# Chosen tokens by indirect DMA with a fifteenth weight slot, gate rows on four column groups, and a last feed-forward group added chunk by chunk

## The chip, the cores and the metric

The kernel runs on one core of a Trainium2 chip, as one program. The metric is device time in microseconds (us); the lower the better. The time before is the median of three runs.

## The reference

Two transformer blocks run one after the other on 512 tokens of width 1024, all in f32. The first is a token mixer (a gated scan, a convolution and attention, merged) followed by an expert-choice feed-forward. The second is pooling and a gated delta rule, cross attention, and a plain feed-forward. The parts that the change touches are these:

```python
def expert_choice_ffn(h, router_w, w_gate, w_up, w_down):
    cap = CAPACITY_FACTOR * n // N_EXPERTS          # 64 tokens for each of 16 experts
    aff = jax.nn.softmax((h @ router_w).astype(jnp.float32), axis=-1)
    w_sel, idx = lax.top_k(aff.transpose(0, 2, 1), cap)
    xs = jax.vmap(lambda hb, ib: hb[ib])(h, idx)
    hid = jax.nn.silu(jnp.einsum('becd,edf->becf', xs, w_gate)) * jnp.einsum('becd,edf->becf', xs, w_up)
    ys = jnp.einsum('becf,efd->becd', hid, w_down) * w_sel[..., None].astype(h.dtype)
    return jax.vmap(lambda yb, ib: jnp.zeros((n, d), h.dtype).at[ib.reshape(-1)].add(yb.reshape(-1, d)))(ys, idx)
...
        proj = hn @ w_in[l]                          # second block
        b = proj[..., P + 4 * W:P + 4 * W + H]       # gate rows: 4 columns
        a = proj[..., P + 4 * W + H:]                # and 4 more
...
        h = h + sqrelu_mlp(rmsnorm_2(h, norm_mlp_g[l]), w_up[l], w_down[l])
    return rmsnorm_2(h, final_norm_g)
```

## The kernel before

Every engine has one program, a list of steps at the end of the kernel (PE_STEPS, DVE_STEPS, ACT_STEPS, SP_STEPS, POOL_STEPS), and semaphores order them. Nothing is planned by cost: an engine runs its list in the order written, and a wait holds all that is behind it. TensorE is PE in the rows, VectorE DVE, ScalarE ACT, SyncE SP.

Weights come through one queue, SP's (`WeightStream.load`, line 164), unit by unit into slots. A unit waits until TensorE has counted up `weights_used` past the unit that had the slot before. For the experts there are fourteen slots of 1024 KB (`SLOTS`), eight in the ring and six in the columns of three branches that are done by then. A pair of experts takes 24 units (gate, up, down; four quarters; two experts), eight pairs 192.

`dve_router` computes affinities, turns them to 16 rows of 512 and finds the 64 largest of each row in eight rounds (line 1982 finds eight, line 1984 replaces them). It then makes of the replaced places a running count, the slot of each token (lines 1987 to 1993). `pe_router` turns that to tokens by experts, and `dve_hot` compares it with the slot numbers: `hot` holds one-hot columns of a pair's 2 x 64 tokens, `whot` the same times the affinity. `pe_gather` (line 2026) multiplies the tokens' rows `h2tok` by `hot`, four matmuls for each of eight chunks, in two halves; `act_gather` (line 2034) scales and shifts. `pe_hot_turn` (line 2045) and `act_hot_turn` turn `whot` for the way back.

`pe_experts` runs the pairs. A quarter of a matrix is eight matmuls for two experts side by side on 64 columns each (line 2169, x16 in the rows, since an f32 matmul stands as two). The way back, `pe_scatter` (line 2071), is one matmul for each of eight chunks and is mixed into the next pair's gate and up quarters; `dve_scatter` adds it to the stream. The gather of the next pair stands between the down quarters:

```python
                    pe_expert_quarter(pe, i, 2, q, 4, lambda e, k: e_hidT[:, k, CAP * e:CAP * e + CAP])
                    if q < 2 and i < PAIRS - 1:
                        pe_gather(pe, i + 1, q)
                    if q == 2:
                        pe_hot_turn(pe, i)
```

`pe_in2` is the second block's first projection. Its gate rows are eight matmuls with 36 columns (line 2356), one for each chunk of the width, then come pool products 2 and 3 (`product`, line 2347), the final norm's sum, the spread of the gate rows over the partitions (`pe_rows_spread`, lines 2385 and 2390), the pool mixes (`mix_pool`, line 2405) and the products of keys, queries and values. `act_in2` makes sigmoid, softplus and the spread's copy of them; `act_qkv_copy` (line 2449) takes each product out of PSUM, and `act_qkv_silu`, in turn with it, waits for VectorE's convolution. `dve_in2` scans the rows, runs pool 0 and the final scalings (line 2297), copies the turned columns (line 2491), and runs pools 1 to 3 before the convolutions (line 2552 on).

In `dve_mlp` the last down group is multiplied by the norm's factor (line 3284) and added to the stream (line 3286), two chunks at a time; ScalarE's squares (line 536) and TensorE's sums for the last norm (line 3316) follow.

Of the kernel before, what the change touches and what calls it, by code (L numbers as in the profile page):

```python
# [6 lines left out]
I32 = mybir.dt.int32  # L7
ALU = mybir.AluOpType
# [176 lines left out]
def mixed_block_kernel(nc, A, out):  # L185

    ctx = ExitStack()
    with ctx:
        sems = {}

        def sem(name):
# [5 lines left out]
            "pe_once": ['rows1_turned', 'rows_turned', 'router_bias', 'aff_turned', 'slots_turned', 'rows2', 'fin_sum', 'spread', 'columns'],  # L197
            "act_once": ['c_exp', 'aff_exp', 'dt_added', 'row_ln', 'fin_root', 'spread_copied', 'decays', 'row_exp'],
            "dve_once": ['silu_c', 'ht_sums', 'ct_sums', 'router_scaled', 'logits_out', 'logits_shifted', 'affinity', 'slots_row', 'mix_columns', 'pool_scaled', 'mix_folded', 'pools_rooted', 'fin_folded', 'row_sums', 'columns_copied', 'd_factors', 'differences', 'queries_out', 'q_decayed'],
# [12 lines left out]
        arena = ctx.enter_context(nc.sbuf_tensor("arena", [P, COLS], F32))  # L212
        psum = ctx.enter_context(nc.psum_tensor("psum", [P, 8, BANK], F32))
# [60 lines left out]
        ws = WeightStream([sem(f"weights_full_{u}") for u in range(14)], sem("weights_used"))  # L274
# [1491 lines left out]

        QUADS = [(0, 0), (0, 1), (3, 1), (2, 0), (1, 0), (2, 1), (3, 0)]
# [76 lines left out]
        hot = [pairwise.take(LT, P) for _ in range(2)]  # L1844
        xs = [ex.take(KC, P) for _ in range(2)]
        whot = [ex.take(LT, P) for _ in range(2)]
# [4 lines left out]
        slotT = rt.take(LT, NE)  # L1851
# [7 lines left out]
        top8 = rt.take(8, 8)  # L1859

# [40 lines left out]
        def pe_router(pe):  # L1901
# [34 lines left out]
        def act_router(act):  # L1936
            await_once(act, "logits_shifted")
            act.activation(aff, aff, ACT.Exp).then_inc(once("aff_exp"), 1)
            for at_, n in enumerate(HTOK_ORDER):
                act.wait_ge(sem("htok"), at_ + 1)  # L1940
                act.activation(h2tok[:, n // 2, (n % 2) * 512:(n % 2) * 512 + 512], psum[:, n % 4, :], ACT.Identity,
                               scale=r_col[:, n // 2:n // 2 + 1]).then_inc(sem("htok_out"), 1)

        def dve_router(dve):
# [36 lines left out]
            for r in range(CAP // 8):  # L1981
                dve.max(top8[0:NE, r, :], work[r % 2])
                dve.drain()
                dve.match_replace(work[(r + 1) % 2], top8[0:NE, r, :], work[r % 2], -1.0)
                dve.drain()
            chosen = row_b[0:NE, :]
            dve.tensor_scalar(chosen, work[0], 0.0, None, ALU.is_lt)
            dve.drain()
            dve.tensor_tensor_scan(row_work[0:NE, :], chosen, chosen, 0.0, ALU.add, ALU.max)
            dve.drain()  # L1990
            dve.tensor_tensor(row_work[0:NE, :], row_work[0:NE, :], chosen, ALU.mult)
            dve.drain()
            dve.tensor_scalar(row_a[0:NE, :], row_work[0:NE, :], 1.0, None, ALU.subtract).then_inc(once("slots_row"), 1)
            await_once(dve, "slots_turned")
            dve.tensor_copy(slotT, psum[:, 7, 0:LT * NE].rearrange("p (t e) -> p t e", t=LT))
            dve.drain()
            dve_hot(dve, 0)

        def dve_hot(dve, i):

            if i >= 2:
                dve.wait_ge(sem("gathered"), 2 * (i - 1))
                dve.wait_ge(sem("hot_turned"), i - 1)
            for t in range(LT):
                dve.tensor_tensor(hot[i % 2][:, t, :].rearrange("p (e c) -> p e c", e=2), bmid(slots, 2),
                                  bcast(slotT[:, t, 2 * i:2 * i + 2], CAP), ALU.is_equal)
            dve.drain()
# [344 lines left out]
        def pe_in2(pe):  # L2352
# [14 lines left out]
            for n in range(8):  # L2367
# [3 lines left out]
                if n == 0:  # L2371
                    mix_pool(pe, 1)
# [1048 lines left out]
```

## Time and profile before

| what | before |
|---|---|
| median of 3 runs | 2751.68 us (2750.51 to 2752.56) |
| profiled execution, its own time | 2754.7 us |
| its span | 2752.9 us |
| mean granted TensorE clock | 0.989 |
| TensorE busy | 2667.6 us (97%) |
| VectorE busy | 1303.1 us (47%) |
| ScalarE busy | 560.8 us (20%) |
| DMA, mean over the span | 136 GB/s |
| DMA packets | 328720, 374.66 MB |

The table is of the whole span; a stage can have another limit. A window gives, for a stretch, the busy time and instructions of TensorE, its weight loads, VectorE, ScalarE and POOL, then the granted clock of TensorE (1.00 is 2.4 GHz, 0.50 is 1.2 GHz) and what the DMA engines moved. The chain of waits is the chain of work that ended last. In a timeline the bracket behind a row is the time in which its engine was idle before it, with what ended that.

### The profile page before, as it was taken

To read this page: it belongs to the slowest core of one execution; us is meant where nothing else is said; L and a number is where in the kernel's file an instruction comes from. 1 tells how busy PE (TensorE), PEld (TensorE's weight loads), DVE (VectorE), ACT (ScalarE), POOL (GpSimd) and SP (SyncE) were. 2 spreads that over 40 slices of the span, in tenths; PEclk is the share of its full clock that TensorE was granted. 3 is DMA by queue.
4 is the path that set the end of the run, shared out by engine and by line. 5 is a ranking of instruction groups with operands and counts; after the bars stand their busy time and mean duration, and the time that the engine had idled before them with its cause. 6 is when DMAs were issued, how large, how long until landed. Compare 5 with 4: busy or idle time off the path is not lost.

```text
span 2752.9 us, 33182 instructions
## 1 busy us (share of the span) xinstructions
PE 2667.6 (97%) x13084; PEld 1873.1 (68%) x13084; DVE 1303.1 (47%) x2417; ACT 560.8 (20%) x942; POOL 170.4 (6%) x140
## 2 busy tenths in 40 slices
PE   6999999999899999999799999999999999999998
PEld 3788888887667666787443333334595877888887
DVE  4255665655465666645311111146473335654654
ACT  3121212222234344311111010122322113000001
POOL 0122211220000000232000000000000000000000
PEclk9999999999999999999899999999999999999999
DMA  9721212211111121235799999952103421233231
GB/s 334 236 62 53 61 43 56 61 30 38 39 47 54 54 62 42 82 90 178 281 409 409 409 409 409 409 178 61 31 1 87 132 73 47 77 92 92 80 89 46
DMA packets 328720, 374.66 MB, mean 136 GB/s; under 512 B 11073, under 2 KB 274070, under 8 KB 325270
## 3 DMA queue, kind: packets, MB, share of 16 engines
q1 hardware_dynamic: 328326, 371.93, 39.8%
q8 instruction: 84, 1.38, 0.2%
q10 hardware_dynamic: 272, 1.05, 0.1%
q14 instruction: 38, 0.31, 0.0%
HBM read 370.85 MB, written 2.10 MB: 135 GB/s over the span
## 4 chain that ended last, share of the span: by engine, by line
PE 89%; DVE 5%; DMA 2%; DVEq 1%; ACT 1%; issue 1%; SPq 0%; ACTq 0%; POOLq 0%; POOL 0%
PE psum L1782 29%; PE psum L2169 12%; PE psum L1462 7%; PE psum L2347 5%; PE psum L720 3%; PE psum L1129 2%; PE psum L2071 2%; PE psum L2026 2%; PE psum L815 2%; PE psum L728 2%; PE psum L2885 2%; PE psum L705 2%; PE psum L1318 2%; PE psum L1370 2%; PE psum L1347 2%; PE psum L2967 1%
## 5 line engine op out<-in xcount | busy, mean ns | idle before, releaser
L1782 PE MATMUL psum<-arena 128*128 128x256 f32 x4144 | 908.6, 378 | 1.9 <-DVEq L1805 1.1
L1782 PEld LDWEIGHTS psum<-arena 128*128 128x128 f32 x4144 | 777.8, 189 | 121.0 <-issue 10.0
L2169 PE MATMUL psum<-arena 128*64 128x512 f32 x1536 | 347.8, 597 | 5.1 <-DMA arena<-in_w_down 3.5
L2169 PEld LDWEIGHTS psum<-arena 128*64 128x64 f32 x1536 | 103.4, 136 | 220.8 <-issue 217.2
L1462 PE MATMUL psum<-arena 128*128 128x256 f32 x896 | 206.6, 381 | 0.0
L1462 PEld LDWEIGHTS psum<-arena 128*128 128x128 f32 x896 | 164.7, 189 | 32.5 <-issue 11.7
L1814 DVE TENSOR_TENSOR arena<-psum,arena 128x256 f32<-128x256 f32 x66 | 28.1, 425 | 303.0 <-ACT arena L1827 183.5
L2076 DVE SCALAR_TENSOR_TENSOR arena<-psum,arena 128x512 f32<-128x512 f32 x64 | 48.1, 751 | 233.0 <-PE psum L2071 232.5
L2347 PE MATMUL psum<-arena 128*128 128x512 f32 (+1 forms) x416 | 157.5, 536 | 0.0
L2347 PEld LDWEIGHTS psum<-arena 128*128 128x128 f32 x416 | 79.8, 193 | 75.1 <-issue 70.8
L1789 POOL TENSOR_TENSOR arena<-arena 128x512 f32<-128x512 f32 x34 | 47.3, 1392 | 1090.5 <-DMA arena<-in_w_in 631.3
L1827 ACT ACTIVATE arena<-psum 128x256 f32<-128x256 f32 x32 | 12.3, 385 | 419.2 <-PE psum L1782 419.2
L720 PE MATMUL psum<-arena 128*128 128x128 f32 x768 | 88.5, 275 | 0.0
L720 PEld LDWEIGHTS psum<-arena 128*128 128x128 f32 x768 | 87.0, 192 | 1.7 <-issue 1.7
L1335 ACT ACTIVATE arena<-psum,arena 128x768 f32<-128x768 f32 x64 | 57.5, 899 | 124.5 <-DVE arena L1329 124.4
L1129 PE MATMUL psum<-arena 128*128 128x512 f32 (+1 forms) x192 | 78.2, 559 | 0.0
L1327 DVE TENSOR_REDUCE arena<-psum 128x1 f32<-128x768 f32 x64 | 61.3, 958 | 24.9 <-PE psum L1318 23.1
L845 DVE TENSOR_TENSOR arena<-arena 128x768 f32<-128x768 f32 (+6 forms) x56 | 26.0, 465 | 99.3 <-PE psum L815 96.4
L815 PEld LDWEIGHTS psum<-arena 128*128 128x128 f32 x448 | 60.9, 190 | 17.5 <-DVEq L860 14.2
L815 PE MATMUL psum<-arena 128*128 128x128 f32 x448 | 65.9, 289 | 6.4 <-DVEq L860 5.1
L1357 ACT ACTIVATE arena<-psum 128x768 f32<-128x768 f32 x64 | 49.6, 811 | 99.6 <-PE psum L1347 98.7
L2071 PE MATMUL psum<-arena 128*128 128x512 f32 x128 | 69.8, 633 | 0.0
(407 smaller groups left out, 3294.7 us busy)
## 6 DMA issues: line engine op xcount, KB each, us to landing
arena<-in_w_gate SPq DMA_DIRECT2D x64, 1024.0 KB, 18.4
arena<-in_w_up SPq DMA_DIRECT2D x64, 1024.0 KB, 18.4
arena<-in_w_down SPq DMA_DIRECT2D x64, 1024.0 KB, 18.4
arena<-in_w_in SPq DMA_DIRECT2D x120, 512.0 KB, 4.5
arena<-in_ada_w SPq DMA_DIRECT2D x24, 1024.0 KB, 7.3
arena<-in_w_up SPq DMA_DIRECT2D x32, 512.0 KB, 5.4
arena<-in_w_down SPq DMA_DIRECT2D x32, 512.0 KB, 5.2
arena<-in_w_out SPq DMA_DIRECT2D x16, 512.0 KB, 4.0
```

The source lines that it names most:

```text
L705: mm = pe.matmul(psum[:, gates_bank(i), d * C:(d + 1) * C], ws.dst("hg", 4 + d)[:, k, :], HT[:, k, 0:C], start=(k == 0), stop=(k == KC - 1))
L720: mm = pe.matmul(psum[:, bank, t * P:(t + 1) * P], HT[:, k, tile * P:(tile + 1) * P], ws.dst("hg", 6)[:, k, :], start=(k == 0), stop=(k == ...
L728: mm = pe.matmul(psum[:, 0, :], ws.dst("hg", 7)[:, k, :], HT[:, k, C:T], start=(k == 0), stop=(k == KC - 1))
L815: mm = pe.matmul(o, hw_kc[:, t * P:(t + 1) * P], queries, start=True, stop=True)
L1129: mm = pe.matmul(psum[:, item_bank(n), 0:item_cols(n)], ws.dst("attn", u)[:, k, :], x[:, k, :], start=(k == 0), stop=(k == KC - 1))
L1327: dve.tensor_reduce(a_stat[:, half, 0:1], score_banks(half), AX, ALU.max)
L1335: act.activation(a_prob[half], score_banks(half), ACT.Exp, bias=a_stat[:, half, 1:2], scale=SCALE, accum_out=a_stat[:, half, 2:3]).then_in ...
L1462: mm = pe.matmul(psum[:, 6 + phase % 2, at_ * HALF:(at_ + 1) * HALF], w, v, start=(at_ == 0 and j == 0), stop=(j == KC // 2 - 1), skip_gro ...
L1782: mm = pe.matmul(psum[:, base + b, c * HALF:(c + 1) * HALF], w, v, start=(first and q == 0 and m in (0, 2, 3, 4)), stop=(last and q == KC ...
L2071: pe.matmul(psum[:, scatter_bank(i, n), :], ys[i % 2][:, n * P:(n + 1) * P], turned_hot[i % 2], start=True, stop=True)\
L2169: mm = pe.matmul(psum[64 * e:64 * e + 64, bank + n, :], tokens(e, 2 * q + k), w[:, k, 512 * n:512 * n + 512], start=(q == 0 and k == 0), s ...
L2347: mm = pe.matmul(psum[:, bank, 0:n], w[:, k, :], x[:, k, :], start=(k == 0), stop=(k == KC - 1))
```

## The change

The chosen tokens are no longer multiplied out. ScalarE's evacuation of the tokens' rows is followed by four stores to a table `token_rows` in HBM, on ScalarE's queue. Each of the eight rounds also asks for the places of its eight values (`max_index`), and the last replaces nothing. The places and the values are turned to one column per pair. POOL, which had nothing to do here, issues one indirect DMA per pair, which reads 128 rows into one of two buffers; TensorE transposes them, eight transposes per pair. What `pe_hot_turn` turned, VectorE now makes at once by comparing a row of token numbers with the pair's places (`dve_spread`). Half of what held the tokens' rows is the fifteenth slot; SP waits for the stores before it fills it.

The gate rows are computed behind pool product 2, eight columns in four column groups, and one matmul with `row_pick` adds the groups after pool product 3; the first key product comes before the spread. The last down group is multiplied and added one chunk after the other, each with its own signal.

```diff
-        ws = WeightStream([sem(f"weights_full_{u}") for u in range(14)], sem("weights_used"))
+        ws = WeightStream([sem(f"weights_full_{u}") for u in range(15)], sem("weights_used"))
...
+        def sp_await_rows(sp):
+            sp.wait_ge(sem("stored"), 16 * LT)
...
-            await_once(pe, "slots_row")
-            for t in range(LT):
-                mm = pe.transpose(psum[:, 7, t * NE:(t + 1) * NE], row_a[0:NE, t * P:(t + 1) * P], ident[0:NE, 0:NE])
-            mm.then_inc(once("slots_turned"), 1)
+            await_once(pe, "picks")
+            for m, picks in enumerate((pick_at[0:NE, :], top8[0:NE].rearrange("p r j -> p (r j)"))):
+                for e in range(2):
+                    mm = pe.matmul(psum[64 * e:64 * e + 64, 7, PAIRS * m:PAIRS * m + PAIRS], picks,
+                                   ident[0:NE, 0:NE].rearrange("p (i e) -> p e i", e=2)[:, e, :], start=True, stop=True)
+            mm.then_inc(once("picks_turned"), 1)
...
+                if at_ in (2, 3, 5, 7):
+                    t = n // 2
+                    act.wait_ge(sem("htok_out"), at_ + 1)
+                    act.dma_start(token_rows[t * P:(t + 1) * P, :], h2tok[:, t, :]).then_inc(sem("stored"), 16)
...
+        def dve_spread(dve, i):
+
+            dve.tensor_scalar(turned_hot[i % 2], token_row, pick_index[:, 1, i:i + 1], pick_weight[:, i:i + 1],
+                              ALU.is_equal, ALU.mult).then_inc(sem("hot_out"), 1)
+
+        def pool_gather(pool):
+            pool.wait_ge(sem("stored"), 16 * LT)
+            await_once(pool, "picks_out")
+            for i in range(PAIRS):
+                if i >= 2:
+                    pool.wait_ge(sem("gathered"), 2 * (i - 1))
+                pool.indirect_dma_start(token_in[i % 2], None, token_rows,
+                                        bass.IndirectOffsetOnAxis(ap=token_index[:, i:i + 1], axis=0))\
+                    .then_inc(sem(f"rows_in_{i % 2}"), 16)
...
             for k in range(4):
-                for t in range(LT):
-                    mm = pe.matmul(psum[:, 6 + half, k * P:(k + 1) * P], h2tok[:, t, (4 * half + k) * P:(4 * half + k + 1) * P],
-                                   hot[i % 2][:, t, :], start=(t == 0), stop=(t == LT - 1))
+                mm = pe.transpose(psum[:, 6 + half, k * P:(k + 1) * P],
+                                  token_in[i % 2][:, (4 * half + k) * P:(4 * half + k + 1) * P], ident)
...
-        SLOTS = [4, 5, 8, 9, 12, 13, 10, 11, 6, 7, 0, 1, 2, 3]
+        SLOTS = [4, 5, 8, 9, 12, 13, 10, 11, 6, 7, 0, 1, 2, 3, 14]
...
-                    if q == 2:
-                        pe_hot_turn(pe, i)
...
-            pe.wait_ge(sem("gates_in"), 64)
+            pe.wait_ge(sem("gates_in"), 48)
+            product(pe, "pool2", 0, 2, hm, 7, m=n_mix)
             for k in range(KC):
-                normed(pe, n_mix, k)
-                mm = pe.matmul(psum[0:32 + DNH, 6, :], w_ba[:, k, :], hm[:, k, :], start=(k == 0), stop=(k == KC - 1))
-            mm.then_inc(once("rows2"), 1)
+                j = 32 * (k % 4)
+                mm = pe.matmul(psum[j:j + 2 * DNH, 6, :], w_ba[:, k, :], hm[:, k, :], start=(k < 4), stop=(k >= 4))
+            mm.then_inc(once("row_parts"), 1)
             await_once(pe, "pools_rooted")
-            product(pe, "pool2", 0, 2, hm, 0)
+            product(pe, "pool2", 0, 3, hm, 1)
+            await_once(pe, "parts_copied")
+            pe.matmul(psum[0:32 + DNH, 6, :], row_pick, cv_x[1], start=True, stop=True).then_inc(once("rows2"), 1)
             pe_fin_sum(pe, 3)
-            product(pe, "pool2", 0, 3, hm, 1)
+            product(pe, QKV_ORDER[0][0], 0, 0, hm, 0)
...
+                    if j == len(JOBS) - 1:
+                        for c in range(2):
+                            dve.tensor_tensor(oo[:, c, :], oo[:, c, :], work2, ALU.mult)
+                            dve.drain()
+                            dve.tensor_tensor(xx[:, c, :], xx[:, c, :], oo[:, c, :], ALU.add).then_inc(sem("down_out"), 1)
```

VectorE at the router, the last round and what follows it, before:

```order
L1982 MAX arena<-arena 16x8
L1984 MATCH_REPLACE arena<-arena 16x512
L1987 TENSOR_SCALAR arena<-arena 16x512
L1989 SCALAR_TENSOR_TENSOR arena<-arena 16x512
L1991 TENSOR_TENSOR arena<-arena 16x512
L1993 TENSOR_SCALAR arena<-arena 16x512
L1995 COPY arena<-psum 128x64
L2005 TENSOR_TENSOR arena<-arena 128x128 x4
```

and with the change:

```order
L1999 MAX arena<-arena 16x8
L2002 MATCH_REPLACE arena<-arena 16x512
L2003 MAX_INDEX arena<-arena 16x8
L1999 MAX arena<-arena 16x8
L2003 MAX_INDEX arena<-arena 16x8
L2005 CAST arena<-arena 16x64
L2009 CAST arena<-psum 128x8
L2010 COPY arena<-psum 128x8
L2011 COPY arena<-psum 128x8
```

Seven rounds have one instruction more; the count, its two factors and the one-hots are gone, and three small copies stand in their place.

TensorE in `pe_in2`, before:

```order
L2142 MATMUL psum<-arena 128x512 x8
L2356 MATMUL psum<-arena 36x512 x8
L2347 MATMUL psum<-arena 128x512 x8
L2286 MATMUL psum<-arena 128x512
L2347 MATMUL psum<-arena 128x512 x8
L2385 MATMUL psum<-arena 128x512 x4
L2390 MATMUL psum<-arena 128x4 x8
L2405 MATMUL psum<-arena 128x512
```

and with the change:

```order
L2146 MATMUL psum<-arena 128x512 x8
L2355 MATMUL psum<-arena 128x512 x8
L2365 MATMUL psum<-arena 8x512 x8
L2355 MATMUL psum<-arena 128x512 x8
L2370 MATMUL psum<-arena 36x512
L2296 MATMUL psum<-arena 128x512
L2355 MATMUL psum<-arena 128x512 x8
L2396 MATMUL psum<-arena 128x512 x4
L2401 MATMUL psum<-arena 128x4 x8
L2416 MATMUL psum<-arena 128x512
```

Both pool products now stand ahead of the matmul that completes the gate rows (line 2370), and the first key product ahead of the spread (line 2396).

## Rows read from the trace of the kernel before

**Rows 1.** The page's slices: GB/s moved by the DMA engines, 40 equal slices.
```profile
GB/s 334 236 62 53 61 43 56 61 30 38 39 47 54 54 62 42 82 90 178 281 409 409 409 409 409 409 178 61 31 1 87 132 73 47 77 92 92 80 89 46
```

**Rows 2.** Windows of 5 us: length, busy us (instructions) per engine, clock, DMA share, GB/s.
```profile
1325.00:1330.00 5.00, 3.68 (x19) 3.57 (x19) 3.99 (x20) 0.00 (x0) 0.00 (x0) 0.50 0.00 0
...
1340.00:1345.00 5.00, 5.00 (x26) 1.68 (x24) 0.00 (x0) 0.00 (x0) 0.00 (x0) 1.00 0.35 110
...
1345.00:1350.00 5.00, 5.00 (x26) 1.71 (x24) 0.00 (x0) 0.00 (x0) 0.00 (x0) 1.00 1.03 421
```

**Rows 3.** Chain of waits, end of the experts' stage: start, us, what.
```profile
1784.02 20.13 DMA arena<-in_w_down
```

**Rows 4.** Timeline, the last quarter: start, us, engine, line, operation, tiles, count, [idle before].
```profile
1804.29 3.65 PE L2169 MATMUL psum<-arena 128*64 128x512 f32 x16 [2.39 <-DMA arena<-in_w_down]
```

**Rows 5.** Chain of waits, down part of pair 0 and first scatter.
```profile
1370.97 3.77 PE psum L2026 x32
...
1382.10 3.59 PE psum L2169 x16
...
1385.69 0.59 PE psum L2045 x4
...
1393.30 1.06 PE psum L2071 x2
```

**Rows 6.** DMA issues, 1150 to 2000: KB each, median us to landing.
```profile
arena<-in_w_gate SPq DMA_DIRECT2D x64, 1024.0 KB, 18.4
...
arena<-in_w_in SPq DMA_DIRECT2D x24, 512.0 KB, 4.6
```

**Rows 7.** Timeline, VectorE, the router's rounds and what follows them.
```profile
1308.68 0.69 DVE L1982 MAX8 arena<-arena 16x8 f32<-16x512 f32 x1
...
1309.44 0.08 DVE L1984 MATCH_VALUE_LOAD arena<-arena 16x8 f32 x1
...
1309.52 0.67 DVE L1984 MATCH_REPLACE8 arena<-arena 16x512 f32<-16x512 f32 x1
...
1321.61 0.41 DVE L1987 TENSOR_SCALAR arena<-arena 16x512 f32<-16x512 f32 x1
...
1325.26 0.23 DVE L1995 COPY arena<-psum 128x64 f32<-128x64 f32 x1 [0.70 <-PE psum L1926]
```

**Rows 8.** Windows during the first gathers; the clock is the value behind POOL.
```profile
1330.00:1332.00 2.00, 2.00 (x11) 2.00 (x11) 0.61 (x4) 0.00 (x0) 0.00 (x0) 0.50 0.00 0
...
1334.00:1338.00 4.00, 2.60 (x24) 2.41 (x22) 0.00 (x0) 1.93 (x6) 0.00 (x0) 1.00 0.00 0
```

**Rows 9.** Timeline, ScalarE, scaling of the second half of gather 0.
```profile
1336.64 1.51 ACT L2034 ACTIVATE arena<-psum,arena 128x128 f32<-128x128 f32 x4 [2.07 <-PE psum L2026]
```

**Rows 10.** Timeline: router logits (first row), then gate rows to the fourth product.
```profile
1298.15 1.90 PE L1878 MATMUL psum<-arena 128*16 128x512 f32 x12
...
1831.27 7.07 PE L2356 MATMUL psum<-arena 128*36 128x512 f32 x16
...
1849.76 5.39 DVE L2297 SCALAR_TENSOR_TENSOR arena<-arena 128x512 f32<-128x512 f32 x8
...
1857.00 0.27 DVE L2491 COPY arena<-psum 128x16 f32<-128x16 f32 x2 [1.85 <-PE psum L2390]
...
1858.74 2.08 PE L2405 MATMUL psum<-arena 128*128 128x512 f32 x2 [1.78 <-ACT arena L2424]
...
1860.61 9.02 PE L2347 MATMUL psum<-arena 128*128 128x512 f32 x16
...
1880.49 0.58 ACT L2449 ACTIVATE arena<-psum 128x512 f32<-128x512 f32 x1
...
1884.95 13.92 PE L2347 MATMUL psum<-arena 128*128 128x512 f32 x32
```

**Rows 11.** Timeline, VectorE, last feed-forward group.
```profile
2737.32 1.22 DVE L3284 TENSOR_TENSOR arena<-arena 128x1024 f32<-128x1024 f32 x1
...
2738.62 1.23 DVE L3286 TENSOR_TENSOR arena<-arena 128x1024 f32<-128x1024 f32 x1
```

More of the change, by code:

```diff
@@ L1843, in mixed_block_kernel @@
         turned_hot = [pairwise.take(S) for _ in range(2)]
-        hot = [pairwise.take(LT, P) for _ in range(2)]
+        token_row = pairwise.take(S)
+        token_in = yT.rearrange("p k n -> p (k n)")
+        token_in = [token_in[:, D * m:D * m + D] for m in range(2)]
         xs = [ex.take(KC, P) for _ in range(2)]
-        whot = [ex.take(LT, P) for _ in range(2)]
+        ex.take(D)
         rt = Carve(arena, EXTRA[0] + 4096, RING_LO)
@@ L1850, in mixed_block_kernel @@
         aff_st = rt.take(LT, 2)
-        slotT = rt.take(LT, NE)
+        pick_at = rt.take(CAP)
+        pick_index = rt.take(2, PAIRS)
+        pick_weight = rt.take(PAIRS)
         router_s = rt.take(KC, NE)
@@ L1859, in mixed_block_kernel @@
         top8 = rt.take(8, 8)
+        top_at = rt.take(8, 8).bitcast(U32)
+        token_index = pick_index[:, 0, :].bitcast(U32)
         def sp_router(sp):
@@ L1992, in dve_router, with dve_token_row @@
+        def dve_token_row(dve):
+            for j in range(S // CAP):
+                dve.tensor_scalar(token_row[:, CAP * j:CAP * j + CAP], slots, float(CAP * j), None, ALU.add)
             dve.drain()
[L1993 to L1997, printed above, removed]
@@ L2059, in pe_scatter @@
                 pe.wait_ge(sem("ys_out"), i + 1)
+                if i < PAIRS - 1:
+                    pe.wait_ge(sem("gather_out"), 2 * (i + 1) + 1)
+                else:
+                    pe.wait_ge(sem("scatter_out"), KC * (i - 1) + 7)
             if n == 1 and i < PAIRS - 1:
@@ L2224, in dve_experts @@
                     dve_mix_fold(dve, n - 1)
+            dve.memset(psum[:, 6, :], 0.0)
+            dve.memset(row_pick, 0.0)
+            dve.drain()
+            by_row = ident.rearrange("p (j r) -> p r j", r=32)
+            for m in range(2):
+                dve.tensor_reduce(row_pick[:, 32 * m:32 * m + DNH], by_row[:, DNH * m:DNH * m + DNH, :], AX, ALU.add)
+            dve.drain()
         X2 = Carve(arena, HT_LO, HT_LO + 4096).take(KC, S)
@@ L2323, in mixed_block_kernel @@
         cv_x = [dn.take(S) for _ in range(2)]
+        row_pick = dn.take(32 + DNH)
         GATE = slice(32, 32 + DNH)
@@ L2366, in pe_in2 @@
             mix_pool(pe, 0)
-            for n in range(8):
+            for n in range(1, 8):
                 if n >= 2:
@@ L2472, in dve_in2 @@
             dve_fin_fold(dve)
-            dve.wait_ge(sem("gates_in"), 64)
+            done(dve, "pool2", 0, 2)
+            dve.tensor_copy(p_mix[2], psum[:, 7, :])
+            dve.drain()
+            dve.wait_ge(sem("gates_in"), 48)
             dve.wait_ge(sem("pool_in"), 32)
@@ L3298, in dve_mlp @@
                     dve_job_sums(dve, j + 2)
-        n_last = norm(X2, hx, S, None, None, 7, work3, lambda k: ("down_out", k // 2 + 1), True)
+        n_last = norm(X2, hx, S, None, None, 7, work3, lambda k: ("down_out", k // 2 + 1 if k < KC - 1 else KC // 2 + 1), True)
         last_r = work3[:, 0:LT]
```

100 lines of the change are left out of this document (40 added, 60 removed).

## The prediction

> **What bounds the kernel now.** I read the page's slices first, then the windows by stretch, then the chain of waits, then the timeline of the places that the edits touch. The slices [rows 1] show one stretch of six in which the DMA engines stand at 409 GB/s: the experts' stage, from 1338 to 1812 us. Everywhere else TensorE is the busy one.
>
> Around the start of that stage the DMA rate is 0 from 1325 to 1330 and 110 GB/s in 1340 to 1345, then 421 [rows 2]: fourteen units lie in their slots, and nothing more can be loaded before the first quarter of pair 0 frees two of them. 110 GB/s over 5 us is 1.3 us of full rate, so the stream restarts at about 1343.7. From there it never stops: its last unit lands at 1804.15, 20.13 us after its issue [rows 3], and TensorE, after a wait of 2.39 us for it, starts the last quarter at 1804.29 [rows 4]. A unit is 1024 KB [rows 6], 1.0486 MB, or 2.56 us at 409 GB/s, so 20.13 us is a queue of nearly eight. Check: 178 units (192 less 14) x 2.56 = 456.4 us from 1343.7 gives 1800.1; the tail, where the rate sags, adds the other 4 us, and I keep it.
>
> TensorE needs per pair 12 quarters x 3.59 + two gather halves x 3.77 + 8 scatters x 1.06 + 0.59 (turning the weighted one-hots) [rows 5], with two hidden turns of some 0.6 about 61 us; the stream needs 24 x 2.56 = 61.5. Both are full and the stream ends last. So the stage's end is restart of the stream + bytes / 409 GB/s, and TensorE work taken out of it frees nothing.
>
> **The change part by part.**
>
> *Chosen tokens, TensorE.* Per pair 32 gather matmuls of 3.77 a half become 8 transposes; four transposes of this shape cost 0.59 [rows 5], so 2 x 3.77 + 0.59 becomes 2 x 0.59: 6.9 us less. TensorE then needs 54 us per pair against at least 61.5 of the stream. Worth nothing: each quarter waits for its unit instead. What is late next is the stream itself.
>
> *Chosen tokens, DMA.* Each pair now reads 128 rows of 4 KB, 512 KB, half a unit: 1.28 us at 409 GB/s. Gathers 0 and 1 fit into the gap before the restart; the other six run inside the full stream: 6 x 1.28 = +7.7 us. Bounds: 0 if they were free, 6 x 4.6 = 27.6 if each held the engines for the whole landing time of a 512 KB load [rows 6]. That landing time is mostly latency, so I take the bytes. Their own lateness costs nothing: a gather may start when the one two pairs before it has been read, about two pairs (over 100 us) ahead of its use.
>
> *Fifteenth slot.* It is filled before the restart, after the token rows are stored. 177 units instead of 178 remain: -2.56 us. The stores (2 MB, 5.1 us at 409 GB/s) and the fifteenth unit lengthen the first filling from about 1322 to about 1330, still 10 us ahead of the restart: nothing.
>
> *The restart.* It comes at the end of the first quarter. Before, the rounds run from 1308.68 to 1321.61 [rows 7]. Seven rounds get an index search beside the replacement, which I price like the replacement, 0.08 + 0.67 = 0.75; the eighth has it in its place: 1321.6 + 5.2 = 1326.8. Then a small cast 0.3, the turn until its read-back 0.70 [rows 7], three small copies 0.6: 1328.4. The five steps that this replaces ended only at 1326.5. Now the first gather by POOL's queue, which no row shows. Nearest is a 512 KB load, 4.6 us from issue to landing [rows 6]; bounds 1.3 (its bytes alone) and 13.8 (three times the 4.6, if software builds the 128 rows slowly). I take 4.6: 1333.0. Then four transposes at the lower clock, 1.1, and two halves of ScalarE's scaling, 2 x 1.51 [rows 9]: 1337.1, where before the second half ended at 1338.15. But the ten microseconds of gather matmuls before also brought the clock back: granted 0.50 (1.2 GHz) until 1332, 1.00 (2.4 GHz) from 1334 on [rows 8], so that the first quarter ran at the upper level. Now it starts with TensorE idle for most of 25 us, hence at 1.2 GHz, for some 4 to 5 us: +2.1. Net **+1.0** (-3 to +10).
>
> Here the Trainium skill has a price that no row has: DMA: Bandwidth & Descriptors, section "Anatomy of one DMA — SWDGE (gpsimd) path", fits such a DMA as about 2.0 us plus its bytes at 436 GB/s, which is 3.2 us; by it the sum would be 1.4 us lower. No run here shows it yet.
>
> Experts' stage: +7.7 - 2.6 + 1.0 = **+6.1**.
>
> *Gate rows.* Eight matmuls with 36 columns took 7.07 us [rows 10]. On four column groups the router's six of the same length took 1.90 [rows 10], so eight take about 2.0 (up to 2.9), and one summing matmul adds 0.86. TensorE saves 4.2. But pool product 2 (6.88) now stands ahead of them and product 3 behind, before the summing matmul. The rows are ready at 1831.3 + 6.9 + 2.0 + 6.9 + 0.9 = 1848.2 instead of 1838.3: 9.9 later. What follows from them is serial: ScalarE's five steps, VectorE's scan and pool 0, together 11.4 us from 1838.3 to 1849.76, then eight final scalings (5.39), then the copy of the columns (0.27) [rows 10]. Before, VectorE waited for TensorE ahead of that copy (1.85 us) and ended it at 1857.3; now it is the late one, at 1848.2 + 11.4 + 5.4 + 0.3 = 1865.3. TensorE has done the summing matmul, the final norm's sum (0.86) and the first key product (6.88) by 1856.0 and then waits, first for the row sums, and again, longer, for the columns. Mix 0 starts at 1865.5 instead of 1858.74. The 6.8 us are just the product that is already done (6.88): **-0.1** so far, if the clock falls as it did before (2.08 and 9.02 us there, where 0.86 and 6.9 are usual).
>
> VectorE however carries on 6.8 late, minus 0.75 for the pool copy made earlier, plus about 0.9 for mix 1, which now comes behind the second product. Its first convolution is at 1883.9 instead of 1876.9, and ScalarE's copy of the second product, which comes behind the first convolution's SiLU, ends at 1888.1 instead of 1881.1. The fourth product needs that copy and started at 1884.95 [rows 10], a slack of nearly 4. It now starts at 1888.1: **+3.1**. After that VectorE catches up, since its work for one product is less than the product's 6.9 us. Together **+3.0**; bounds -4 (all of TensorE's saving kept) and +6 (the 3 us wait also drops the clock). The memset and the small reductions lie in the 6 us in which VectorE waits for the norm's root: nothing.
>
> *Last group by chunks.* Before, a multiply of 1.22 and an add of 1.23 stood ahead of the first square [rows 11]. By halves of about 0.69 each, chunk 6 is done after 1.45 instead of 2.56, and its square starts 1.1 earlier; chunk 7's ends before the sums of chunk 6. **-1.1** (-1.3 to 0).
>
> **Sum.** +6.1 + 3.0 - 1.1 = +8.0 against the profiled execution's own 2754.7: 2762.7. The median of the runs, 2751.68, lies 3.0 below that execution; moved by as much, **2759.7**, +0.29%. A measurement of this kernel tells 0.2%, 5.5 us, from no change.
>
> **The rivals.**
> 1. *The gathers' bytes cost nothing* (not slower). The point: whether the stage moves weights plus gathers above 409 GB/s. For it: 421 stands once, right after the restart [rows 2]. Against it: no later window goes above 410 for long, and the share is already 1.03. Free gathers: 2759.7 - 7.7 = 2752.0. If the whole stream ran at 421, 180 unit equivalents save 13.2: 2746.5.
> 2. *The first gather is slow.* 8 us more than the 4.6 would shift the restart by as much: 2767.7. For it: a software path, first use. Against: only bounds.
> 3. *Short waits drop the clock.* TensorE will now wait in nearly every quarter. At 1.2 GHz a quarter is 7.2 us, more than the stream's 5.1, so the waits would vanish and the clock return; only what stands behind the last landing would be dearer, the quarter's 3.65 and part of the scatters: +5, 2764.7. The wait of 2.39 us before 1804.29 left the clock up, the quarter took 3.65 [rows 4]; but 1.78 us behind sparse work at 1857 did not [rows 10]. [...]
> 4. *The projection keeps its saving*: -4 instead of +3.0: 2752.7.
>
> **Chances.** Forecast 0.55 (own range 2755 to 2765); rival 1 0.18 (a third of it at the higher rate); rival 2 0.12; rival 3 0.08; rival 4 0.07. Within 0.2% (2746.2 to 2757.2): rivals 1 and 4 mostly, and the low edge of the forecast, 0.27. Faster: the high rate, or gains of 1 and 4 together, 0.10. Slower 0.63. The range from 2749 to 2768 leaves out the high rate and a still slower gather.
>
> **What would show it.** Windows of the stage at 409 GB/s with waits of the quarters for w_gate, w_up and w_down; the last w_down landing about 6 us later; first gather landing within 5 us; gate rows' matmuls about 2 us; a wait of several us of mix 0 for VectorE's columns; the first convolution 7 us later and a 3 us gap before the fourth product; the last square 1.1 us sooner after the add. The prediction is wrong if the DMA rate of the stage is above 415, or if the restart lies more than 3 us from where I put it.

## The result, and the profile after

| what | before | after |
|---|---|---|
| median of 5 runs each | 2750.51 us (2750.01 to 2752.56) | 2764.25 us (2759.41 to 2767.12) |
| ratio of the medians, 95% interval | | 1.0046 [1.0034, 1.0057] |
| profiled execution, its own time | 2754.7 us | 2760.68 us |
| its span, mean granted clock | 2752.9 us, 0.989 | 2758.9 us, 0.986 |

The changed kernel is slower, by 13.7 us where 8.0 were forecast; 2764.25 lies 4.6 above the forecast of 2759.7 and inside its range. The two profiled executions differ by 6.0 only, since that of before lies 3 to 4 us above its kernel's median and that of after 3.6 below its own. So stages are compared from an anchor: R is the start of the first of the eight rounds at the router, 1308.68 before [rows 7], 1304.97 after. Of the change only the first store of token rows lies ahead of R, by 0.5 us; the executions of all kernels here have R from 1302.8 to 1308.7, and most of that spread is there after the first 86 us. From R to the end the traces have 1444.2 us before and 1453.9 after.

The page of after, busy time and GB/s in its 40 slices:

```profile
PE 2613.5 (95%) x12610; PEld 1827.0 (66%) x12610; DVE 1295.8 (47%) x2388; ACT 556.4 (20%) x935; POOL 178.4 (6%) x148
...
GB/s 351 222 57 61 53 53 46 61 30 38 38 62 53 47 54 46 81 89 214 340 409 409 409 409 409 409 163 55 37 1 84 130 77 44 79 92 89 80 92 46
```

54 us of TensorE's work are gone and the time is longer. The experts' stage still stands at 409 GB/s, as in [rows 1]. Windows of after (length, busy us with instructions of PE, PEld, DVE, ACT, POOL, then clock, DMA share, GB/s):

```profile
1325.00:1330.00 5.00, 1.04 (x5) 1.04 (x6) 1.24 (x8) 0.00 (x0) 1.38 (x2) 0.50 0.75 247
1330.00:1335.00 5.00, 2.86 (x11) 1.23 (x11) 0.00 (x0) 4.19 (x9) 0.94 (x1) 0.50 0.34 109
1335.00:1340.00 5.00, 5.00 (x18) 1.45 (x16) 0.00 (x0) 0.00 (x0) 0.00 (x0) 0.61 0.00 2
1340.00:1345.00 5.00, 5.00 (x26) 1.53 (x22) 0.00 (x0) 0.00 (x0) 0.00 (x0) 1.00 0.85 300
...
1400.00:1800.00 400.00, 351.55 (x1456) 122.44 (x1454) 51.47 (x72) 38.76 (x74) 3.76 (x4) 1.00 1.03 409
```

The first quarter (from 1333) runs at 0.50 until about 1339, then the clock is back. From 1400 to 1800 TensorE works 351.55 us of 400, and what it waits for are the weights. The same window of before, and the costliest group of the stage by line (busy, mean ns, idle before and releasers), before and after:

```profile
1400.00:1800.00 400.00, 398.85 (x1861) 154.54 (x1858) 59.29 (x108) 43.39 (x81) 0.00 (x0) 1.00 1.03 409
...
L2169 PE MATMUL psum<-arena 128*64 128x512 f32 x1486 | 336.8, 597 | 1.2 <-DMA arena<-in_w_down 1.2
...
L2173 PE MATMUL psum<-arena 128*64 128x512 f32 x1468 | 334.0, 597 | 48.4 <-DMA arena<-in_w_down 21.5 <-DMA arena<-in_w_gate 17.3 <-DMA arena<-in_w_up 9.7
```

The first gather, in the chain of waits of after (start, us, what):

```profile
1324.35 4.57 DMA arena<-token_rows,arena
...
1328.96 1.13 PE psum L2042 x4
...
1330.12 2.91 ACT arena L2050 x8
...
1333.08 12.11 PE psum L2173 x41
```

It lands 4.57 us after POOL begins to issue it. The fifteenth unit was still on its way then (landed at 1327.30), and the second gather was issued at 1325.74. The steps behind it are those of the working: four transposes at the lower clock 1.13, the scaling 2.91, the first quarter 28.1 us after R where I had 28.4.

The end of the stage, in the same chain. Here stands what the prediction does not have:

```profile
1785.75 18.48 DMA arena<-in_w_down
...
1804.36 3.67 PE psum L2173 x16
1808.04 0.34 SPq L165
...
1808.42 5.51 DMA arena<-in_w_in
...
1813.95 1.23 DVE arena L2221
...
1816.20 3.23 PE psum L2146 x4
...
1831.02 6.87 PE psum L2146 x16
1837.89 2.15 PE psum L2355 x5
```

Before, TensorE went from the last quarter straight into the next projection; here it is idle, because SP issues the first unit of that projection only when the last quarter has ended, at 1808.01. SP's timeline and the chain of before:

```profile
1787.61 18.10 SPq L164 DMA_DIRECT2D arena<-in_w_in  x4
```
```profile
1831.33 3.99 PE psum L2356 x9
```

The way from the last quarter to the gate-row part of the second block is 33.53 us (1804.36 to 1837.89); before it was 27.04 (1804.29 to 1831.33).

TensorE in that part of after (timeline; idle before in brackets), to be read against [rows 10]:

```profile
1837.73 7.04 PE L2355 MATMUL psum<-arena 128*128 128x512 f32 x16
1844.70 1.90 PE L2365 MATMUL psum<-arena 128*8 128x512 f32 x16
1846.53 7.15 PE L2355 MATMUL psum<-arena 128*128 128x512 f32 x16
...
1870.59 2.05 PE L2416 MATMUL psum<-arena 128*128 128x512 f32 x2 [4.18 <-issue]
...
1892.39 15.42 PE L2355 MATMUL psum<-arena 128*128 128x512 f32 x32 [3.15 <-ACT arena L2462]
1907.65 1.02 PE L2416 MATMUL psum<-arena 128*128 128x512 f32 x2
```

The gate rows take 1.90 instead of 7.07. Mix 0 starts 32.9 us into the part (27.5 before), the fourth product 54.7 (53.7 before) after a wait of 3.15 us for ScalarE's copy; then two products take 15.42 instead of 13.92.

At the end (timeline of after), the last group by chunks:

```profile
2744.33 0.69 DVE L3303 TENSOR_TENSOR arena<-arena 128x512 f32<-128x512 f32 x1
2745.09 0.69 DVE L3305 TENSOR_TENSOR arena<-arena 128x512 f32<-128x512 f32 x1
...
2745.82 0.63 ACT L538 ACTIVATE arena<-arena 128x512 f32<-128x512 f32 x1 [4.26 <-DVE arena L3305]
```

The first square starts 1.49 us after the first multiply; before, the add alone ended 2.53 after it (1.30 to its start, and 1.23) [rows 11].

### The profile page after: what moved, and what is told of

It reads as the page before. It is cut to its first block, busy times and chain, and to the rows that moved or that the text cites. A ratio compares the mean times of both kernels' runs of the same rounds, so it can differ in the third digit from the quotient of the medians.

```text
span 2758.9 us, 32179 instructions
## 1 busy us (share of the span) xinstructions
PE 2613.5 (95%) x12610; PEld 1827.0 (66%) x12610; DVE 1295.8 (47%) x2388; ACT 556.4 (20%) x935; POOL 178.4 (6%) x148
## 3 DMA queue, kind: packets, MB, share of 16 engines
q10 hardware_dynamic: 848, 3.15, 0.3%
## 4 chain that ended last, share of the span: by engine, by line
PE 77%; DMA 14%; DVE 5%; DVEq 1%; ACT 1%; issue 1%; SPq 0%; ACTq 0%; POOLq 0%; POOL 0%
PE psum L1787 29%; PE psum L1464 7%; PE psum L2355 5%; PE psum L2173 4%; DMA arena<-in_w_down 4%; DMA arena<-in_w_gate 4%; DMA arena<-in_w_up 4%; PE psum L722 3%; PE psum L1131 2%; PE psum L817 2%; PE psum L730 2%; PE psum L2902 2%; PE psum L707 2%; PE psum L1320 2%; PE psum L1372 2%; PE psum L1349 2%
## 5 line engine op out<-in xcount | busy, mean ns | idle before, releaser
L2173 PEld LDWEIGHTS psum<-arena 128*64 128x64 f32 x1536 | 116.4, 137 | 268.8 <-issue 266.1
L1819 DVE TENSOR_TENSOR arena<-psum,arena 128x256 f32<-128x256 f32 x66 | 28.1, 425 | 304.7 <-ACT arena L1832 184.3
```

What stands on the lines that cost most here:

```text
L2173: mm = pe.matmul(psum[64 * e:64 * e + 64, bank + n, :], tokens(e, 2 * q + k), w[:, k, 512 * n:512 * n + 512], start=(q == 0 and k == 0), s ...
```

## The experiments

All times are medians. Each group of runs had its own runs of the kernel before on the same chip: 2749.45 of 19 runs for the first four rows of the table, 2749.06 of 33 for the next four, 2750.60 of 35 for the last four. "Stage" is the time from SP's first load after a slot has come free to the start of the last quarter. That load stands in SP's timeline, of before and then of after:

```profile
1341.88 0.88 SPq L164 DMA_DIRECT2D arena<-in_w_up  x2
```
```profile
1339.62 0.37 SPq L165 DMA_DIRECT2D arena<-in_w_up  x1
```

So before has R + 33.2 and a stage of 462.4; after R + 34.7 and 464.7.

| run | median (lowest to highest, runs) | ratio to before | stage |
|---|---|---|---|
| after, again | 2763.41 (2759.94 to 2764.70, 5) | 1.0043 [1.0030, 1.0057] | 464.6 |
| after, pool units' semaphores moved | 2758.76 (2755.61 to 2760.95, 6) | 1.0032 [1.0020, 1.0044] | 464.6 |
| after, fourteen slots | 2756.76 (2755.10 to 2759.27, 8) | 1.0028 [1.0017, 1.0038] | 467.5 |
| after, semaphores moved, three gathers only | 2746.95 (2744.40 to 2752.15, 11) | 0.9991 [0.9981, 1.0000] | 458.2 |
| before + gate rows | 2754.51 (2749.60 to 2758.43, 11) | 1.0017 [1.0008, 1.0026] | |
| before + last group by chunks | 2749.36 (2744.10 to 2753.27, 11) | 0.9998 [0.9989, 1.0007] | |
| before + work under the rounds | 2749.01 (2745.27 to 2753.13, 11) | 0.9997 [0.9988, 1.0006] | |
| before + gate rows, rows first | 2751.89 (2747.51 to 2754.27, 11) | 1.0006 [0.9997, 1.0015] | |
| the same, copy ahead of SiLU | 2746.19 (2742.86 to 2750.19, 11) | 0.9983 [0.9974, 0.9991] | |
| the same + last group by chunks | 2745.26 (2741.25 to 2749.29, 12) | 0.9982 [0.9974, 0.9991] | |
| before + tokens by DMA, semaphores moved | 2755.34 (2752.84 to 2756.55, 11) | 1.0017 [1.0009, 1.0026] | 464.8 |
| after, all three mended | 2746.63 (2745.26 to 2749.20, 11) | 0.9990 [0.9981, 0.9998] | |

### After once more

No edit. 

> The changed kernel once more, beside the kernel before, for the spread of its runs (2759.4 to 2767.1 on record, where the kernel before has 2750.0 to 2752.6). If the spread belongs to the change, the ratio comes out between 1.003 and 1.006 again and the runs lie over 4 us apart or more; its profile tells in which stretch they differ. Theory A: the start-up differs (the profile on record began its router rounds at 1304.97, that of before at 1308.68). Theory B: the experts' stage or what stands behind it differs, since the gathers meet the stream at other moments.

2763.41, so the result stands. The chain is the same (last quarter 1803.21, the projection's load for 5.43 us from 1807.27); from R to the end it has 1456.4 us. In this execution two windows of 10 us inside the experts' stage have a granted clock of 0.83, and the rate does not change:

```profile
1550.00:1560.00 10.00, 7.50 (x28) 2.36 (x25) 0.00 (x0) 0.10 (x1) 0.00 (x0) 0.83 1.03 412
...
1610.00:1620.00 10.00, 6.68 (x25) 2.35 (x25) 0.00 (x0) 1.50 (x4) 0.93 (x1) 0.83 1.02 408
```

Such stretches stand in four of the seven traces of kernels with the gathers (here, with fourteen slots, with the tokens alone, with all three mended) and not in the other three. The wait ahead of the first one is 2.42 us, at 1554.50. In after the same quarter, at 1555.70, had the same wait of 2.42 us, and the clock stayed up: 3.66 us.

### The pool units on other semaphores

In `WeightStream.phase` a unit waits for the last unit that overlaps it in memory and for the last one on its semaphore (`slot_last`). The four units of the next projection (`pool2`) stand on semaphores 0 to 3. With fourteen slots the last of the 192 units on them are 178 to 181, with fifteen they are 190 and 191 for 0 and 1: the very last of the stage. The edit leaves the places in memory and moves the semaphores alone.

```diff
-                     [at + u for u in range(4)])
+                     [8, 9, 12, 13] if name == "pool2" else [at + u for u in range(4)])
```

> Changed kernel, but the four pool2 loads use the semaphores of slots 8, 9, 12, 13 instead of 0 to 3, nothing else. Theory: with fifteen slots the last two units of the experts fall on slots 0 and 1, whose semaphores pool2 uses, so its first load is issued only behind the last quarter (1808.04), lands 5.5 us later and holds VectorE and then TensorE. If so, the load is issued before the last landing, TensorE goes from the last quarter to the gate rows' stage in 27 us instead of 33.5, and the kernel gains 5 to 6.5 us on the changed one. Rival: the 6.5 us come from contention or the lower clock there; then nothing moves by more than 2 us.

2758.76, 4.7 less than after in the same group of runs (3.0 by the two ratios). Its chain:

```profile
1804.09 3.65 PE psum L2173 x16
1807.74 3.63 PE psum L2077 x8
1811.38 1.72 PE psum L2146 x4
...
1831.13 6.88 PE psum L2355 x16
```

27.04 us, as before. The wait was this one, and nothing else of the 6.5 is left. In the trace it is worth 6.1 to 6.5, between the medians 4.7; their intervals are about 3.5 us either way.

### Fourteen slots

```diff
-        SLOTS = [4, 5, 8, 9, 12, 13, 10, 11, 6, 7, 0, 1, 2, 3, 14]
+        SLOTS = [4, 5, 8, 9, 12, 13, 10, 11, 6, 7, 0, 1, 2, 3]
```

> Changed kernel with fourteen slots as before, indirect gathers kept. One unit more in the stream costs 2.6 us, and the late pool2 loads go away (5 to 6.5 us), so it is 2.5 to 4 us faster than the changed kernel: the fifteenth slot costs more than it gives. Rival: the slot is worth its 2.6 us and the lateness has another cause; then it is 2.6 us slower.

The fifteenth slot taken out of the changed kernel makes it 6.6 us faster: the stage gets 2.9 longer and the wait above is gone (2756.76 against 2763.41; 4.1 by the two ratios). The traces give 3.2 to 3.6 for it. The medians do not show what the slot brings: with the slot and the semaphores moved the kernel took 2758.76, 2.0 more, where the stage says 2.9 less. The intervals are too wide to tell.

### Three gathers instead of eight

On the kernel with the semaphores moved; pairs 3 to 7 work on rows that were not gathered for them.

```diff
-            for i in range(PAIRS):
+            for i in range(3):
...
-            if half == 0:
+            if half == 0 and i < 3:
```

> As e1_pool_sems, but only the first three gathers are read; the pairs behind use what lies in the buffers, so five indirect DMAs (2.6 MB) and their waits are left out and the output of five pairs is not the reference's. Theory (bytes bound the stage): the last landing comes 5 x 1.28 = 6.4 us earlier against the start of the first quarter than in e1_pool_sems, and the time falls by 6.4. Rival (the gathers ride beside the stream for nothing): no change within 1 us. Rival (each gather disturbs the stream by more than its bytes): 10 us or more.

The stage is 6.4 us shorter, and the gathers are five of 1.27. Only five, since the third is already issued in the gap ahead of the restart. The last quarter of this run and of the one with all gathers, by their chains:

```profile
1796.98 3.19 PE psum L2173 x13
```

The latter started at 1804.09. Between the medians lie 11.8 us, 5.4 more than the stage gives. The two profiled executions lie 6.0 apart (2750.99 and 2756.95), as the stage says, with the same mean clock of 0.986; so no trace holds the other 5 us, and their cause stays open.

### Gate rows alone, on the kernel before

The whole part of the change in `pe_in2`, `act_in2`, `dve_in2` and `dve_pool`, nothing else. 

> Kernel before with the gate-row part of the change alone (rows behind pool product 2 on four column groups, summing matmul behind product 3, first key product ahead of the spread). Theory A, the prediction's step: TensorE saves 4.2 us, but VectorE's convolutions come 7 us later, the fourth product waits 3 us, and the clock can fall in that wait: +2.5 to +4.5 us on the kernel before. Rival: the saving is kept: -3 to -4 us.

5.4 us slower. TensorE's timeline:

```profile
1863.94 2.04 PE L2413 MATMUL psum<-arena 128*128 128x512 f32 x2 [4.32 <-issue]
...
1885.28 15.11 PE L2352 MATMUL psum<-arena 128*128 128x512 f32 x31 [2.81 <-ACT arena L2459]
...
1900.65 1.02 PE L2413 MATMUL psum<-arena 128*128 128x512 f32 x2
```

The row of 15.11 lacks the last matmul of its pair, which lies outside this view; the whole pair of products (x32) took 15.54. The part starts at 1830.75; the mix at 1900.65 is 69.9 us into it, before 67.4 (1898.71 and 1831.27). So the trace shows +2.5 of the median's +5.4, whose interval reaches from 2.2 to 7.2.

### Last group by chunks alone

The diff is the last one of the change. 

> Kernel before with the last down group by chunks alone. Theory: the first square of the last pair starts 1.1 us sooner behind the last quad's sum, and so does the end: -1.1 us in the trace, 0.04%, too little for the medians. Rival: the sums of the last norm wait for the other chunk anyway: 0.

The trace has the same rows as after, 1.50 us from the first multiply to the first square, and the last sums end 5.75 us behind that multiply, before 6.82. A difference of 1.1 us is below what 11 runs tell: 0.9998 [0.9989, 1.0007].

### TensorE busy under the rounds

```diff
+            for _ in range(11):
+                pe.matmul(psum[:, 5, :], ident, XT[:, 0, :], start=True, stop=True)
             await_once(pe, "slots_row")
```

> Kernel before plus eleven matmuls of 128x512 into an unused bank while TensorE waits for the router's rounds; they add work whose result nobody reads. Theory: the clock is at its upper level when the first gather starts, the 10.07 us of gather 0 become 7.6, the first quarter and with it the restart of the stream come 2.5 us earlier, and the whole kernel gains that, 2.5 us. Rival 1: the matmuls run past the end of the rounds and delay the gather: 0 or up to 2 us slower. Rival 2: the stage's end does not hang on the restart: 0.

No gain. The windows of its trace:

```profile
1309.00:1322.00 13.00, 9.23 (x25) 3.91 (x23) 11.03 (x23) 0.00 (x0) 0.00 (x0) 1.00 0.77 306
1323.00:1329.00 6.00, 5.74 (x27) 5.74 (x28) 3.65 (x18) 0.00 (x0) 0.00 (x0) 0.50 0.00 0
```

The clock was up while the added matmuls ran. They ended 3.7 us before the next work, four short matmuls at 1321.52; at 1323 the clock was down, and the first gather took 10.35 as ever. The edit did not reach its aim, so it says nothing on what a warm first quarter is worth.

### Gate rows first

Before pool product 2, with the summing matmul before product 3, so that the chain on ScalarE and VectorE starts as early as it did.

```diff
-            product(pe, "pool2", 0, 2, hm, 7, m=n_mix)
             for k in range(KC):
+                normed(pe, n_mix, k)
...
+            product(pe, "pool2", 0, 2, hm, 7)
+            await_once(pe, "parts_copied")
+            pe.matmul(psum[0:32 + DNH, 6, :], row_pick, cv_x[1], start=True, stop=True).then_inc(once("rows2"), 1)
             await_once(pe, "pools_rooted")
             product(pe, "pool2", 0, 3, hm, 1)
```

> As e5_in2_alone, but the gate rows' eight matmuls come first, then pool product 2, then the summing matmul, then pool product 3. Theory: what hurt was that the rows were complete only behind both pool products, 9.9 us later than before; now they are complete 2.8 us later, VectorE's convolutions come about 2.5 us later, within the slack of 4, the fourth product does not wait, and TensorE keeps its 4.2 us: -3.5 to -4.5 us on the kernel before, 6 to 8 us less than e5_in2_alone. Rival: the wait comes from elsewhere (mix 1 behind the second product): no more than 2 us less than e5_in2_alone.

2.6 us less than with the rows late, still 2.8 above before; neither is clear of the intervals. TensorE and ScalarE ahead of the fourth product:

```profile
1829.92 1.90 PE L2362 MATMUL psum<-arena 128*8 128x512 f32 x16
...
1881.71 16.75 PE L2352 MATMUL psum<-arena 128*128 128x512 f32 x32 [3.32 <-ACT arena L2460]
...
1898.30 1.02 PE L2414 MATMUL psum<-arena 128*128 128x512 f32 x2
```
```profile
1880.54 0.63 ACT L2465 ACTIVATE arena<-arena 128x512 f32<-128x512 f32 x1 [11.70 <-DVEq L2572]
1881.08 0.58 ACT L2460 ACTIVATE arena<-psum 128x512 f32<-128x512 f32 x1
```

TensorE is sooner and waits for the same copy, 3.32 us; behind the wait two products take 16.75, not 13.9, and the window shows the clock:

```profile
1882.00:1889.00 7.00, 7.00 (x11) 2.94 (x11) 6.43 (x9) 1.11 (x2) 0.00 (x0) 0.63 0.01 2
```

The fourth product starts 51.8 into the part (53.7 before), its pair ends at 68.4 (67.4). What was saved is given back in the clock. The second product had been done since 1869.6; its copy (L2460) stands in ScalarE's queue behind the SiLU of the first (L2465), and that waits 11.70 us for VectorE's pools and its first convolution.

### Copy ahead of the SiLU

```diff
+            act_qkv_copy(act, 0)
             for n in range(8):
-                act_qkv_copy(act, n)
+                if n < 7:
+                    act_qkv_copy(act, n + 1)
                 act_qkv_silu(act, n)
```

> The kernel before with the gate-row edit, the gate rows first (as in the run with the rows first) and ScalarE copying product n+1 out of PSUM before it takes the SiLU of product n. Theory A (the fourth product waits only because ScalarE's copy of the second product stands in its queue behind the first SiLU, which waits for VectorE's pools and first convolution): the copy comes at once after the second product, about 40 us after the stage's start, the fourth product starts when TensorE is free, 48 to 49 us after the stage's start (51.7 with the rows first, 53.8 before), no wait over 0.5 us ahead of it, the next two products take 13.8 and the stage is about 4 to 5 us shorter than before: ratio 0.9982 to 0.9990. Theory B (VectorE's convolutions bound this place whatever the order): one of the following copies waits for a convolution instead, and the time stays within 1.5 us of before.

2746.19, 4.4 below before (0.9983 [0.9974, 0.9991]). ScalarE, then TensorE:

```profile
1871.89 0.60 ACT L2462 ACTIVATE arena<-psum 128x512 f32<-128x512 f32 x1 [3.64 <-PE psum L2352]
```
```profile
1830.62 1.90 PE L2362 MATMUL psum<-arena 128*8 128x512 f32 x16
...
1880.28 13.92 PE L2352 MATMUL psum<-arena 128*128 128x512 f32 x32
1894.04 1.02 PE L2414 MATMUL psum<-arena 128*128 128x512 f32 x2
```

The copy comes as soon as the product ends; no idle time stands ahead of the fourth product, 49.7 into the part, and the pair ends at 63.4 instead of 67.4: 4.0 saved in the trace, nearly all of the 4.2 that TensorE is rid of in the gate rows. Theory A holds; VectorE's convolutions were not the bound. The copy ahead of the SiLU without the gate rows' edit was not run; before, TensorE had no wait ahead of the fourth product [rows 10] that it could have taken away.

### The version that beats both

The same with the last group by chunks. 

> The same as the run with the copy first, plus the last feed-forward group chunk by chunk. Theory A: 1.1 us less than that run, so 5 to 6 us less than before, ratio 0.9978 to 0.9984. Theory B (the chunk edit is hidden or lost): the same as the run with the copy first.

2745.26 (0.9982 [0.9974, 0.9991]): 5.3 below before, and by the two ratios (0.9982 and 1.0046) some 17.6 below after. The 0.9 between this and the last run is as forecast, but within the intervals.

### Chosen tokens alone

The changed kernel with the gate rows and the last group of before, semaphores moved. 

> The changed kernel with only the chosen tokens by indirect DMA and the fifteenth slot kept; gate rows and last group as before, and the four pool units on semaphores whose last users are long gone. Theory A (the three parts add up): the last quarter starts about 3.8 us later than before relative to the rounds, nothing more, so +3 to +5 us, ratio 1.0011 to 1.0018. Theory B (the parts do not add up, more comes from clock falls among the waits for weights): +7 us or more.

+4.7 us. Stage 464.8, 2.4 more than before. The restart lies at R + 32.9 here and at R + 34.7 in after, though the first quarter starts alike (R + 27.9 and R + 28.1): here the clock is at 1.00 from 1336, 3.4 us into that quarter, in after from 1339, 5.9 us into it. The last quarter comes at R + 497.8 (1802.40 less 1304.64) and R + 499.4, before R + 495.6. So the tokens cost 2.2 to 3.8 in the traces.

### After, all three mended

After with the semaphores moved, the rows first and the copy ahead of the SiLU. 

> The changed kernel with the pool units' semaphores, the gate rows first and the copy before the SiLU. Theory A: the 3.8 us of the experts' stage less 4 to 5 of the projection less 1.1 of the last group: within 2 us of before, ratio 0.9993 to 1.0004. Theory B (the clock falls oftener with the new waits, and eats what is saved): 3 us or more above before.

2746.63 (0.9990 [0.9981, 0.9998]), 4.0 below before, somewhat better than the theory's bound of 2; the sum of parts, 4.7 - 4.4 - 1.1 = -0.8, lies inside the interval of -5.2 to -0.5. It doesn't beat the version without the gathers (2745.26).

## Why the prediction was right in its sign and short in its size

The parts, measured one by one, make the whole: tokens by DMA +4.7, gate rows +5.4, last group -1.1 (by its trace), the shared semaphore +4.7, together 13.7 of the 13.7 measured. With intervals of 2 to 3.5 us on each (and 3.0 for the last term by the ratios) the closeness is luck; that the fourth term is needed is not. The traces, too, tell single terms only stage by stage: from the gate rows to the end the same code took 918.6 to 923.0 us (before, tokens alone, work under the rounds). It is luck as well that the forecast came within 4.6 us: the experts' stage was put 2.3 to 3.9 too high, which made up for part of the missing term. Point by point:

- **The bound.** Right. 409 GB/s in every window, waits of 48.4 us for the three weights, and 54 us of TensorE's work without a gain.
- **Chosen tokens, DMA.** The mechanism and the price of one, 1.28, were right (1.27 measured); five ran inside the stream, not six, so 6.4 and not 7.7: the third gather was issued at 1331.21, ahead of the restart. Rival 1, free bytes, is refuted by the three gathers.
- **Chosen tokens, TensorE, "worth nothing".** 1.2 us too low: the stage without gathers in it is 458.2, and with the slot's 2.9 given back 461.2, where before it was 462.4. What is left for the difference is that TensorE and stream were both full before; that is argued, no run isolates it.
- **Fifteenth slot, -2.56.** 2.9 measured. But this is **the step that failed**: I wrote that the stores and the fifteenth unit cost "nothing", and looked only at how the first filling grows. I counted the units per slot and not which unit comes last on which semaphore; with 15 in place of 14 the last two of the stage fall on those that the next projection's loads wait for. The loads were moved from before the end of the stage to behind it, with a landing of 5.51 us in the open and a slow clock behind (four matmuls took 3.23 us, 1.72 in the run with the semaphores moved). Measured: +6.1 to +6.5 in the traces, +4.7 between medians, more than the slot brings.
- **The restart, +1.0.** +1.5 in the trace of after, -0.3 where only the tokens are changed, and between the two in the other traces; what differs is how soon the clock comes back. The first gather's landing, 4.57, is what I took (4.6). The Trainium skill's page DMA: Bandwidth & Descriptors, section "Anatomy of one DMA — SWDGE (gpsimd) path", gives about 2.0 us plus the bytes at 436 GB/s, an estimate of 3.2 us for these 512 KB; the trace does not agree. Rival 2 did not come.
- **Experts' stage together, +6.1.** 2.2 to 3.8 in the traces, 4.7 in the median of the tokens alone.
- **Gate rows, +3.0.** The mechanism is right row by row: 1.90 (2.0 forecast), mix 0 32.9 us into the part (34.2 forecast), a wait of 3.15 ahead of the fourth product (3 forecast). The fourth product itself started only 1.0 later than before, not 3.1, since TensorE got to it 2.2 sooner than before (51.5 us into the part against 53.7), where I had 0.1. Mis-sized was what comes behind the wait: I put the clock's fall into the bound of +6, and it came in every trace with that wait (15.42 to 17.01 for two products instead of 13.92). +2.5 in the trace, +5.4 in the median. Rival 4 is refuted; that the saving can be kept took two more edits.
- **Last group, -1.1.** Right in the trace, too small for the medians.
- **Rival 3, short waits drop the clock.** Inside the stage it happens rarely and costs nothing, since the stream is the bound: the clock of 1400 to 1800 is 1.00 in after with 12% of TensorE's time spent waiting, and the two windows at 0.83 in the second run keep 408 to 412. The Trainium skill's page TensorE: Matmul & The Clock Gate, section "HAM oscillation — how this bites in real kernels", tells of an engine throttled again in every tile, where the wait for the DMA is longer than the tile's matmuls; here the waits (0.5 to 2.4 us) are shorter than the quarters (3.65 us), and no run shows that case. Outside the stage a single wait of 3 us cost 1.5 to 3.1 us.

What would have told me before: the list of units per semaphore for the phase after the experts, and the chain's rows between the last quarter and the projection, in which no DMA stood. It stood in none of my views because it cost nothing before; the edit of a ring's length is a move of every load behind it.

## What to carry to other kernels

When a ring of buffers gets one slot more, write down for the last round, and for the next phase that shares its semaphores, who waits for whom: one unit less to load can put a full landing time on the path. Where an engine saves work but then waits, look at what stands ahead of the awaited instruction in its own queue: here a copy could have been made 11 us sooner but stood behind an activation that waited for something else, and only with the two turned round was the edit's saving kept. And TensorE's work is worth nothing, or next to nothing, in a stage that a stream of weights bounds.

## What the runs showed of the hardware

- An indirect DMA of 128 rows of 4 KB landed 4.31 us after POOL began to issue it with nothing else in flight (the third gather of after, at 1331.21), 4.57 beside a weight unit and the second gather, and 7.4 to 8.3 inside the weight stream, where it cost 1.27 us of the stream's time. A second queue beside the weights' left the rate of the stage at 408 to 412 GB/s in all windows shown here.
- A wait of 2.8 to 3.4 us of TensorE ahead of the fourth product was followed by a stretch at the lower clock in all seven traces that have it there (after twice, its three variants with the rows late, and the two on the kernel before); one of 3.7 us under the rounds as well. In the experts' stage a wait of 2.42 us at the same quarter was followed by a fall in one run of the changed kernel and not in the other. A wait of 2.39 us near the stage's end left the clock up before (the quarter behind it took 3.65 [rows 4]) and not in the run with the last group alone (5.35).
- The rounds took 2.24 us each with the index search, 1.62 without (12.93 for eight [rows 7]); the search itself takes as long as the replacement, 0.67.
